# Query weights ahead of the gate weights in the ring, and the last turned rows of each head behind the next piece of work

## The chip, the core and the metric

The kernel runs on one core of a Trainium2 chip. The core has five engines that run on their own instruction lists and meet at semaphores: TensorE (PE, matrix products, PEld for its weight loads), VectorE (DVE), ScalarE (ACT), GpSimd (POOL) and SyncE (SP, which here only issues DMAs). Each engine takes its list strictly in order, so an instruction that waits holds up everything behind it. The metric is the time of one execution in microseconds on the device; the kernel before takes 2796.95 us (median of three runs, 2794.47 to 2798.68).

## The reference

The program computes two blocks in a row on 512 tokens of width 1024. The change touches only the start and the end of the heads of the first mixer of the second block, an mLSTM with 4 heads, on 512 latent and 256 context tokens:

```python
q, k, v, o, z, g = jnp.split(h @ w_in, ML_SPLITS, axis=-1)        # for latent and context rows
...                                                               # g: 16 gate columns, q and k: 256 per head
hc, st = mlstm_scan(qc, kc, vc, li_c, lf_c, zero)                 # both directions; the state goes on
hl, _ = mlstm_scan(ql, kl, vl, li_l, lf_l, st)
...
hn = _merge_heads(_head_rms(h_sum, head_g)).astype(o.dtype)       # norm over the 512 columns of a head
return (jax.nn.sigmoid(o) * hn * jax.nn.silu(z)) @ w_out
```

The input `h` is the first block's output after its final RMS norm, and after the second block's own norm and modulation.

## The kernel before, in words

**Split products.** Every large weight matrix is cut into units of at most 128 x 1024 numbers, each loaded by SP into a ring of five raw slots (`wring`). ACT rounds a unit to its high part (`wh`, L1086), POOL subtracts to get the low part (`wl`, L2234), and TensorE makes three products of high and low parts (L515 in `project`, L535 in `product`). `wh` and `wl` have only **three slots**. The function `split` on ACT waits, before it writes unit number n of the ring, until TensorE has reported the unit n - 3 as used. The order of the units is that of `weight_jobs()`, and it decides which unit waits for which. The order in which ACT and POOL work on them is written out by hand in their own programs and has to follow it.

**The start of the mixer.** After the last down projection of the first block (`dn`, to about 1410 us) TensorE makes the context half of the gate columns, takes the sum of squares of the latent rows (`norm(("mL", 0))`, a product with ones), makes the context half of the queries of head 0, takes the same for the final norm (`norm(("fin", 0))`), and then, k-tile by k-tile as the normed rows arrive, the latent halves of gates and queries (L535). Behind it stands `project_qk(0)`, the keys of head 0 (weights `("mqk", 0, 1)`, L515). Its claims wait until ACT has copied the two query tiles out of PSUM (`mqk`, L1429), since they use the same banks.

ACT at this place: squares, `root(("mL", 0))` (L1128, L1132), the high parts of the normed rows (L1114), `root(("fin", 0))` (L1128, L1132 again), then the softplus of the forget gates (L1383 to L1388), which waits for DVE's `glf` (L1918), then `split(("mqk", 0, 1))`, then the copies of the queries (L1429). DVE: the normed rows (L1679, L1687), the final norm of the first block, which needs ACT's root (L1702, 8 tiles), four memsets, the gates out of PSUM (L1916, L1918), and after the softplus the running sums and maxima of the gates (L1922 to L1945, `gfm`), for which TensorE waits after `project_qk(0)`.

**A head.** For each head: queries and keys, the row maxima of the decay matrix spread over the partitions (L876 and L565, two pairs, one for each direction, banks 4, 5 and 6, 7), the values, the scores, and in `head_pv` the product with the values, six row tiles for two directions (L855). Each row tile is normed by DVE, ACT and POOL (L1959 to L1968, L1402 to L1417, L2337) and then turned by four transposes of TensorE (L862); ACT copies the result out (L1420). The turned rows of tile t - 1 stand behind the products of tile t; those of the last tile stand at the end, with nothing ahead of them. `head_pv(h - 1)` for odd h stands behind `project_qk(h)`, and is followed by the two pairs of L876 and L565; `head_pv(h)` for odd h is followed by the first output gate unit, `("oz", 8 * f)`. An `("oz", j)` is two units of weights and four outputs: o for context and latent rows, z for both; each output runs through both units.

## Time and profile before

| what | value |
|---|---|
| median of three runs | 2796.95 us |
| the profiled execution | 2804.22 us |
| its span, first to last instruction | 2802.2 us |
| mean granted clock of TensorE | 0.967 of full speed |
| TensorE busy | 2602.1 us (93%) |
| chain that ended last | PE 85%, DVE 5%, POOL 4%, ACT 4% |

The busy shares are an average over the whole program; what matters for this change are the few places where TensorE stands still in the mLSTM part. A granted clock of 1.00 is 2.4 GHz, 0.50 is 1.2 GHz.

### The profile page before, as it was taken

How to read it: one execution, taken by the hardware profiler on the slowest of the kernel's cores; microseconds unless marked ns; L12 is line 12 of the kernel's file. 1: busy time of each engine (PE TensorE's matmuls, PEld its weight loads, DVE VectorE, ACT ScalarE, POOL GpSimd, SP SyncE). 2: the span in 40 equal slices, each digit the busy share in tenths (PEclk: the TensorE clock that was granted, in tenths of full speed). 3: DMA queues.
4: the chain of work that ended last, by engine and by line, in shares of the span. 5: the costliest groups of instructions: out<-in, count | busy, mean ns of one | idle time of the engine just before them, and what ended most of it. 6: DMA issues, size and time to landing. Idle time of an engine off the chain costs nothing.

```text
span 2802.2 us, 33854 instructions
## 1 busy us (share of the span) xinstructions
PE 2602.1 (93%) x13182; PEld 2113.0 (75%) x13182; DVE 1123.0 (40%) x2055; ACT 992.7 (35%) x1814; POOL 977.5 (35%) x515
## 2 busy tenths in 40 slices
PE   5999899999999989999989899989999998898888
PEld 4775678888777567888868778878877887786666
DVE  2135489520213658952161122420121242455564
ACT  3334344432334534443232222221222222344442
POOL 4321345765432225576532222222222223321121
PEclk9999899999999989999999999999999999899999
DMA  4211245222311115523221000211100111120000
GB/s 167 68 35 53 68 155 191 94 94 94 112 65 35 61 61 184 177 94 109 92 72 38 23 31 31 68 51 57 47 21 31 38 61 53 56 63 28 24 30 30
DMA packets 54013, 200.57 MB, mean 72 GB/s; under 512 B 5984, under 2 KB 5984, under 8 KB 52960
## 3 DMA queue, kind: packets, MB, share of 16 engines
q1 hardware_dynamic: 51696, 188.65, 20.0%
q10 hardware_dynamic: 2160, 9.76, 1.0%
q8 instruction: 106, 1.74, 0.3%
q14 instruction: 51, 0.42, 0.0%
HBM read 196.29 MB, written 2.10 MB: 71 GB/s over the span
## 4 chain that ended last, share of the span: by engine, by line
PE 85%; DVE 5%; POOL 4%; ACT 4%; issue 2%; DMA 0%; ACTq 0%; POOLq 0%; DVEq 0%
PE ps L515 53%; PE ps L535 12%; PE ps L565 8%; PE ps L855 5%; PE ps L713 3%; POOL wl L2234 2%; POOL norm_acc L2247 1%; PE ps L728 1%; PE ps L1049 1%; DVE norm_sq L1679 1%; ACT wh L1086 1%; PE ps L715 0%; POOL norm_sq L2337 0%; PE ps L862 0%; PE ps L1034 0%
## 5 line engine op out<-in xcount | busy, mean ns | idle before, releaser
L2234 POOL TENSOR_TENSOR wl<-wring,wh 128x1024 fp32r<-128x1024 f32 (+1 forms) x305 | 762.4, 2500 | 1395.1 <-ACT wh L1086 1383.9
L1086 ACT ACTIVATE wh<-wring 128x1024 fp32r<-128x1024 f32 (+1 forms) x305 | 316.8, 1042 | 743.9 <-PE ps L515 736.9
L515 PE MATMUL ps<-hh,wh 128*128 128x512 f32 x1200 | 471.6, 393 | 20.3 <-DVE hl L1691 16.0
L515 PE MATMUL ps<-hl,wh 128*128 128x512 f32 x1200 | 469.8, 392 | 0.0
L515 PE MATMUL ps<-hh,wl 128*128 128x512 f32 x1200 | 469.5, 391 | 0.0
L515 PEld LDWEIGHTS ps<-hh,wh 128*128 128x128 f32 x1200 | 227.2, 189 | 72.4 <-DVE hl L1691 15.0
L515 PEld LDWEIGHTS ps<-hh,wl 128*128 128x128 f32 x1200 | 227.0, 189 | 47.8
L515 PEld LDWEIGHTS ps<-hl,wh 128*128 128x128 f32 x1200 | 227.1, 189 | 46.0 <-issue 0.5
L565 PE MATMUL ps<-arena 128*128 128x64 f32 (+2 forms) x720 | 186.3, 395 | 14.1 <-ACT arena L1297 5.8
L1716 DVE CUSTOM_DVE_ANT_0 arena<-arena 128x1024 f32<-128x1024 f32 x96 | 185.8, 1935 | 9.0 <-DVE arena L1892 0.5
L535 PE MATMUL ps<-hh,wh 128*128 128x512 f32 (+1 forms) x408 | 171.1, 419 | 7.6 <-DVE hl L2215 3.4
L565 PEld LDWEIGHTS ps<-arena 128*128 128x128 f32 x720 | 108.7, 196 | 85.0 <-issue 57.3
L535 PE MATMUL ps<-hh,wl 128*128 128x512 f32 (+1 forms) x408 | 162.0, 397 | 0.0
L535 PE MATMUL ps<-hl,wh 128*128 128x512 f32 (+1 forms) x408 | 161.5, 396 | 0.0
L855 PE MATMUL ps<-arena 128*128 128x258 f32 (+1 forms) x672 | 150.0, 380 | 2.4 <-DVE arena L1992 2.4
L1829 DVE CUSTOM_DVE_ANT_0 arena<-ps,arena 128x128 f32<-128x128 f32 (+3 forms) x128 | 62.7, 490 | 207.1 <-PE ps L715 111.9
L855 PEld LDWEIGHTS ps<-arena 128*128 128x128 f32 x672 | 125.0, 189 | 23.0 <-issue 4.0
L1288 ACT ACTIVATE arena<-arena,st 128x128 f32<-128x128 f32 (+3 forms) x128 | 71.8, 561 | 192.3 <-DVE st L1829 192.2
L515 PE MATMUL ps<-gu_h,wh 128*128 128x512 f32 x352 | 139.7, 397 | 0.0
L515 PE MATMUL ps<-gu_l,wh 128*128 128x512 f32 x352 | 139.5, 396 | 0.0
L515 PE MATMUL ps<-gu_h,wl 128*128 128x512 f32 x352 | 139.5, 396 | 0.0
L515 PE MATMUL ps<-wh,hh 128*128 128x256 f32 x416 | 121.2, 291 | 6.1 <-POOL wl L2234 4.3
(279 smaller groups left out, 4956.0 us busy)
## 6 DMA issues: line engine op xcount, KB each, us to landing
wring<-wts SPq DMA_DIRECT2D x290, 512.0 KB, 3.5
arena<-wts SPq DMA_DIRECT2D x48, 512.0 KB, 4.3
wring<-wts SPq DMA_DIRECT2D x16, 384.0 KB, 2.9
xL<-xt SPq DMA_DIRECT2D x1, 2048.0 KB, 9.7
arena<-tab SPq DMA_DIRECT2D x1, 2048.0 KB, 16.9
arena<-cv ACTq DMA_DIRECT2D x2, 1024.0 KB, 5.6
arena<-tab ACTq DMA_DIRECT2D x1, 2048.0 KB, 9.0
out_t<-xL ACTq DMA_DIRECT2D x8, 256.0 KB, 2.0
```

The costliest lines, as they stand in the source:

```text
L515: mm = nc.tensor.matmul(o[0], a, b, start=start and k == first and j == 0, stop=stop and k == last and j == 2)
L535: mm = nc.tensor.matmul(dst, a, b, start=start and x == 0 and i == 0 and j == 0, stop=stop and x == len(us) - 1 and i == kn - 1 and j == 2)
L565: last = nc.tensor.matmul(dst, a, b, start=start and i == 0, stop=stop and i == len(pairs) - 1)
L713: last = nc.tensor.matmul(ps[:, s % 3, 0:ke], a, b, start=True, stop=kind != "fox")
L728: last = nc.tensor.transpose(ps[:, 3 + tb, 128 * j:128 * j + 128], sbuf[:, u % 4, 128 * j:128 * j + 128], idn)
L855: last = nc.tensor.matmul(ps[:, b + half, 0:c1 - c0], arena[:, eo:eo + 128], mvt[:, s, c0:c1], start=i == 0, stop=i == len(src) - 1)
L1049: last = nc.tensor.transpose(ps[:, 4 + j // 4, 128 * (j % 4):128 * (j % 4) + 128], asb[:, u % 4, 128 * j:128 * j + 128], idn)
L1086: nc.scalar.activation(wh[:, sn % SPLIT_SLOTS, :kn * w], raw(u)[:, :kn * w], ACT.Copy).then_inc(act_done, tick("act", ("hi", u)))
L1288: nc.scalar.activation(sbuf[:, s % 4, 0:ke], sbuf[:, s % 4, 0:ke], ACT.Exp, scale=-1.0, bias=mx1[:, s % 16:s % 16 + 1], accum_out=rs1[:, s ...
L1716: V.tensor_tensor_reduce(out=ada_dump, in0=raw(u), in1=crow[:, j, :], scale=1.0, scalar=0.0, op0=ALU.mult, op1=ALU.add, accum_out=modv[:, ...
L1829: V.tensor_tensor_reduce(out=sbuf[:, s % 4, 0:ke], in0=ps[:, s % 3, 0:ke], in1=bias, scale=-scale, scalar=3e38, op0=ALU.add, op1=ALU.min, ...
L2234: G.tensor_tensor(wl[:, sn % SPLIT_SLOTS, :kn * w], raw(u)[:, :kn * w], wh[:, sn % SPLIT_SLOTS, :kn * w].bitcast(F32), ALU.subtract).then_inc(
```

## The change

Three things are moved, nothing is computed otherwise.

1. In the order of the ring the gate unit goes behind the two query units of head 0. TensorE makes the first unit's half of the context queries, the sum of squares, the second half, and then the context gates. ACT splits `("mqk", 0, 0)` at the end of the down projection and the gate unit between the last squares, and `("mqk", 0, 1)` ahead of `root(("fin", 0))` instead of behind the softplus. POOL follows.
2. For even heads the transposes of the last row tile move from the end of `head_pv` to between the two pairs of L876 and L565 (`last_rows(h - 1, 0)`).
3. For odd heads they move into the middle of the first `("oz", j)`, between o and z, and to bank 4 (`last_rows(h, 4)`). That first `("oz", j)` is written out by `product` instead of `project`; both its units are reported as used by its last matmul.

```diff
@@ weight_jobs
-    add(("gate",), "ml_w_in_2", 0, 0, KT,
-        [(ML_G, 4), (None, 28), (ML_G + 8, 4), (None, 28), (ML_G + 4, 4), (None, 28), (ML_G + 12, 4)])
     for f in range(2):
         for h in (2 * f, 2 * f + 1):
             add(("mqk", h, 0), "ml_w_in_2", 0, 0, KT, [(256 * h, 256)])
+            if h == 0:
+                add(("gate",), "ml_w_in_2", 0, 0, KT, [(ML_G, 4), (None, 28), (ML_G + 8, 4), (None, 28),
+                                                       (ML_G + 4, 4), (None, 28), (ML_G + 12, 4)])
             add(("mqk", h, 1), "ml_w_in_2", 0, 0, KT, [(1024 + 256 * h, 256)])
@@ TensorE, start of the mixer
-            claim([4, 5], "dve", "glf")
-            product(ps[0:100, 4, 256:512], rows(gate_all, *hc), [gate_unit])
-            norm(("mL", 0))
             for i in range(2):
                 claim([2 * i, 2 * i + 1], "act", "mqk", 0, i)
             for u in query_units:
                 for i in range(2):
                     product(ps[:, 2 * i, 256:512], rows(side(i), *hc), [u], start=u is query_units[0],
                             stop=u is query_units[1])
+                if u is query_units[0]:
+                    norm(("mL", 0))
+            claim([4, 5], "dve", "glf")
+            product(ps[0:100, 4, 256:512], rows(gate_all, *hc), [gate_unit])
             norm(("fin", 0))
@@ TensorE, head_pv and what follows
+            def last_rows(h, b):
+
+                pe.wait_ge(pool_done, at("pool", "hn", h, NA - 1))
+                claim([b], "act", "ht", h, NA - 1)
+                for j in range(4):
+                    last = nc.tensor.transpose(ps[:, b, 128 * j:128 * j + 128],
+                                               hb[:, (NA - 1) % 2, 128 * j:128 * j + 128], idn)
+                last.then_inc(pe_done, tick("pe", ("ht", h, NA - 1)))
+
             def head_pv(h):
 
-                for t in range(NA + 1):
+                for t in range(NA):
...
                 for d in range(2):
+                    if d and h % 2:
+                        last_rows(h - 1, 0)
                     b, r = 4 + 2 * d, ROW0[d] + h
...
                     claim([b + 2, b + 3], "dve", "zz", j)
+                    if j == 8 * f:
+                        for i, key in enumerate((("o", j), ("z", j))):
+                            us = views(("oz", j))
+                            product(ps[:, 2 * i, 256:512], rows(side(i), *hc), us)
+                            product(ps[:, 2 * i + 1, :], lat(side(i)), us, key,
+                                    *([("used", x[0]) for x in us] if i else []))
+                            if i == 0:
+                                last_rows(h, 4)
+                        continue
                     project(("oz", j), both(b // 2, P, side(0), ("o", j)) + both(b // 2 + 1, P, side(1), ("z", j)))
@@ ACT
-                            split(("gate",) if last else ("cq", l + 1))
+                            split(("mqk", 0, 0) if last else ("cq", l + 1))
...
-            split(("mqk", 0, 0), first)
             square_both(6)
             square(("mL", 0), 7, ("xd", DEPTH - 1), fgn[:, 7:8])
-            split(("mqk", 0, 0), second)
+            split(("gate",))
             square(("fin", 0), 7, ("xd", DEPTH - 1))
             root(("mL", 0))
             high(("mL", 0), hH, 0)
+            split(("mqk", 0, 1))
             root(("fin", 0))
...
+                        b = t % 2 if t < NA else 4 * (h % 2)
                         nc.scalar.activation(hn[:, 4 * (h % 2):4 * (h % 2) + 4, 128 * (t - 1):128 * t],
-                                             ps[:, t % 2, :].rearrange("p (a b) -> p a b", a=4), ACT.Copy).then_inc(
+                                             ps[:, b, :].rearrange("p (a b) -> p a b", a=4), ACT.Copy).then_inc(
...
-                    if m % 2 == 0:
+                    if m % 2 == 0 and h + m:
                         split(("mqk", h, 1) if m == 0 else ("mv", h, 0))
@@ POOL
-                            split(("gate",) if last else ("cq", l + 1))
+                            split(("mqk", 0, 0) if last else ("cq", l + 1))
...
-            split(("mqk", 0, 0), slice(0, 1))
             accumulate(("mL", 0), 6)
             accumulate(("fin", 0), 6)
             accumulate(("mL", 0), 7)
-            split(("mqk", 0, 0), slice(1, 2))
+            split(("gate",))
             accumulate(("fin", 0), 7)
```

The first place is ACT at the start of the mixer. 128x800 is the gate unit, `hh` the normed rows, 128x512 from `ps` the root of the final norm, 36x768 the softplus, 128x768 the copies of queries and keys. Before:

```order
L1114 ACTIVATE hh<-norm_sq,mod 128x512 x8
L1128 ACTIVATE arena<-ps,prmt 128x512
L1132 ACTIVATE arena<-arena 128x512
L1383 ACTIVATE arena<-arena 36x768
L1385 ACTIVATE arena<-arena 36x768
L1388 ACTIVATE arena<-arena 36x768
L1086 ACTIVATE wh<-wring 128x1024 x2
L1429 ACTIVATE arena<-ps 128x768 x2
```

And now, in the same stretch (line numbers are those of the changed kernel, about 20 higher):

```order
L1134 ACTIVATE hh<-norm_sq,mod 128x512 x8
L1106 ACTIVATE wh<-wring 128x1024 x2
L1148 ACTIVATE arena<-ps,prmt 128x512
L1152 ACTIVATE arena<-arena 128x512
L1403 ACTIVATE arena<-arena 36x768
L1405 ACTIVATE arena<-arena 36x768
L1408 ACTIVATE arena<-arena 36x768
L1450 ACTIVATE arena<-ps 128x768 x2
```

The two splits of the key weights moved ahead of the root of the final norm; the copies of the queries stay behind the softplus.

The second place is TensorE at the end of head 0 (products of the last row tile, L855 before and L864 now; transposes from `norm_sq`; the two pairs from `arena` and `prmt`; then the values of head 1). Before:

```order
L855 MATMUL ps<-arena 128x256 x3
L855 MATMUL ps<-arena 128x258 x3
L862 MATMUL ps<-prmt,norm_sq 128x128 x8
L876 MATMUL ps<-arena,prmt 128x256
L565 MATMUL ps<-arena,prmt 128x512
L876 MATMUL ps<-arena,prmt 128x256
L565 MATMUL ps<-arena,prmt 128x512
L515 MATMUL ps<-wh,hc_h 128x256
```

Now:

```order
L864 MATMUL ps<-arena 128x256 x3
L864 MATMUL ps<-arena 128x258 x3
L871 MATMUL ps<-prmt,norm_sq 128x128 x4
L887 MATMUL ps<-arena,prmt 128x256
L566 MATMUL ps<-arena,prmt 128x512
L847 MATMUL ps<-prmt,norm_sq 128x128 x4
L887 MATMUL ps<-arena,prmt 128x256
L566 MATMUL ps<-arena,prmt 128x512
L516 MATMUL ps<-wh,hc_h 128x256
```

Of the eight transposes the last four went behind the first pair.

The third place is TensorE at the end of head 1, where `("oz", 0)` follows (L515 before; L536 now, since it is written out by `product`). Before:

```order
L855 MATMUL ps<-arena 128x256 x3
L855 MATMUL ps<-arena 128x258 x3
L862 MATMUL ps<-prmt,norm_sq 128x128 x8
L515 MATMUL ps<-hc_h,wh 128x256
L515 MATMUL ps<-hc_l,wh 128x256
L515 MATMUL ps<-hc_h,wl 128x256
```

Now:

```order
L864 MATMUL ps<-arena 128x256 x3
L864 MATMUL ps<-arena 128x258 x3
L871 MATMUL ps<-prmt,norm_sq 128x128 x4
L536 MATMUL ps<-hc_h,wh 128x256
...
L536 MATMUL ps<-hh,wl 128x512
L847 MATMUL ps<-prmt,norm_sq 128x128 x4
L536 MATMUL ps<-hc_h,wh 128x256
```

In the rows left out stand the rest of the 48 matmuls of o; the last four transposes now follow them, ahead of z.

## Rows read from the trace of the kernel before

**Rows 1.** The page: the chain that ended last, share of the span by engine.

```profile
PE 85%; DVE 5%; POOL 4%; ACT 4%; issue 2%; DMA 0%; ACTq 0%; POOLq 0%; DVEq 0%
```

**Rows 2.** TensorE's waits: line, who waited for, us in total, times, longest us.

```profile
PE ps L862 <- POOL norm_sq L2337: 23.7, 8, 4.2
```

**Rows 3.** Timeline of TensorE, 1410 to 1449 us: start, duration, instruction, idle time before.

```profile
1414.67 0.70 PE L565 MATMUL ps<-norm_acc,ones 128*128 128x512 f32 x1 [1.59 <-POOL norm_acc L2247]
...
1438.37 0.39 PE L535 MATMUL ps<-hh,wl 128*128 128x512 f32 x1
...
1448.82 0.55 PE L515 MATMUL ps<-hc_h,wh 128*128 128x256 f32 x1 [10.06 <-POOL wl L2234]
```

**Rows 4.** Timeline of ScalarE, 1406 to 1447 us.

```profile
1429.04 0.67 ACT L1128 ACTIVATE arena<-ps,prmt 128x512 f32<-128x512 f32 x1
...
1441.17 0.84 ACT L1383 ACTIVATE arena<-arena 36x768 f32<-36x768 f32 x1 [10.79 <-DVE arena L1918]
...
1443.67 1.99 ACT L1086 ACTIVATE wh<-wring 128x1024 fp32r<-128x1024 f32 x2
...
1445.56 1.48 ACT L1429 ACTIVATE arena<-ps 128x768 f32<-128x768 f32 x2
```

**Rows 5.** Timeline of VectorE and GpSimd, same stretch and what follows.

```profile
1430.41 5.39 DVE L1702 SCALAR_TENSOR_TENSOR xL<-xL,prmt,arena 128x512 f32<-128x512 f32 x8 [0.49 <-ACT arena L1132]
...
1460.30 0.55 DVE L1945 TENSOR_SCALAR arena<-arena 36x768 f32<-36x768 f32 x1
...
1444.79 6.60 POOL L2234 TENSOR_TENSOR wl<-wring,wh 128x1024 fp32r<-128x1024 f32 x2 [25.66 <-ACT wh L1086]
```

**Rows 6.** Timeline of ScalarE and TensorE, end of head 0.

```profile
1599.75 0.69 ACT L1402 ACTIVATE norm_sq<-ps,st 128x512 f32<-128x512 f32 x1 [3.06 <-DVE st L1963]
...
1601.40 0.60 PE L862 MATMUL ps<-prmt,norm_sq 128*128 128x128 f32 x4
...
1606.15 1.11 PE L862 MATMUL ps<-prmt,norm_sq 128*128 128x128 f32 x4 [4.16 <-POOL norm_sq L2337]
...
1607.20 1.22 PE L876 MATMUL ps<-arena,prmt 36*128 36x256 f32 x2
...
1609.92 1.06 PE L876 MATMUL ps<-arena,prmt 36*128 36x256 f32 x2
...
1612.61 0.58 PE L515 MATMUL ps<-wh,hc_h 128*128 128x256 f32 x1
```

**Rows 7.** Timeline of TensorE and ScalarE, end of head 1.

```profile
1704.78 0.60 PE L862 MATMUL ps<-prmt,norm_sq 128*128 128x128 f32 x4
...
1707.73 0.58 ACT L1420 ACTIVATE arena<-ps 128x512 f32<-128x512 f32 x1
...
1711.33 0.58 PE L515 MATMUL ps<-hc_h,wh 128*128 128x256 f32 x1 [0.69 <-ACT arena L1420]
```

**Rows 8.** The first output gates: TensorE, ScalarE, GpSimd.

```profile
1727.17 1.06 ACT L1086 ACTIVATE wh<-wring 128x1024 fp32r<-128x1024 f32 x1 [14.94 <-PE ps L515]
...
1728.31 2.40 POOL L2234 TENSOR_TENSOR wl<-wring,wh 128x1024 fp32r<-128x1024 f32 x1 [13.63 <-ACT wh L1086]
...
1729.40 0.39 PE L515 MATMUL ps<-hh,wl 128*128 128x512 f32 x1
```

**Rows 9.** Stretches: length, busy time of each engine, granted clock (PEclk), DMA.

```profile
1472.00:1473.00 1.00, 1.00 (x4) 0.26 (x2) 1.00 (x4) 0.00 (x0) 0.00 (x0) 0.79 0.00 0
1562.00:1569.00 7.00, 5.22 (x26) 3.93 (x25) 3.90 (x14) 3.33 (x9) 1.63 (x2) 1.00 0.24 76
1708.00:1709.00 1.00, 0.00 (x0) 0.00 (x0) 0.00 (x0) 0.31 (x1) 1.00 (x1) 0.55 0.00 0
1714.00:1715.00 1.00, 1.00 (x7) 1.00 (x6) 0.00 (x0) 0.00 (x0) 0.67 (x1) 0.54 0.00 0
1846.00:1848.00 2.00, 0.00 (x0) 0.00 (x0) 2.00 (x2) 1.54 (x2) 0.89 (x1) 1.00 0.14 20
1848.00:1849.00 1.00, 0.00 (x0) 0.00 (x0) 0.97 (x2) 0.00 (x0) 0.00 (x0) 0.52 0.74 229
```

More of the change, by code:

```diff
@@ L838, in project_v @@
                 project(key, outs, claims=lambda t: claim([t % 4], "act", "mv2", h, j, t) if t >= 4 else None)
+            def last_rows(h, b):
[5 more added lines that the diff above has]
+                last.then_inc(pe_done, tick("pe", ("ht", h, NA - 1)))
             def head_pv(h):
-                for t in range(NA + 1):
+                for t in range(NA):
                     for d in range(2):
-                        if t == NA:
-                            break
                         b = 4 + 2 * d
```

## The prediction, made before the changed kernel ran

> **What bounds the kernel now.** I read the chain of waits first: TensorE holds 85% of it [rows 1], so only what makes TensorE stop or slow down counts. Then its waits, summed: 23.7 us in eight waits for normed rows [rows 2]; the longest single one outside the norms is 10.06 us for the low part of a weight unit [rows 3]. Then the timeline at these places. The 10.06 us stand at the start of the mixer: the last matmul of the latent queries ends at 1438.76, the first of head 0's keys starts at 1448.82 [rows 3]. The row blames GpSimd, but that engine only starts at 1444.79 [rows 5], after ScalarE's split at 1443.67 [rows 4]; and the split stood behind the softplus, which had itself waited 10.79 us for VectorE [rows 4]. The reader should see one more thing: the copies of the queries, 1445.56 to 1447.04 [rows 4], are behind the softplus too, and the keys' banks wait for them. So two things release the keys, the weights at about 1448.7 and the banks at 1447.1. Of the eight waits for normed rows four, at the last tile of each head, are 4.16 us long [rows 6]; the other four, at the first tile, share what is left of the 23.7, 1.8 each.
>
> **Start of the mixer, up to the queries.** The gate unit's low part gives way to a second full one ahead of the sum of squares. A full unit costs GpSimd 2.40 us [rows 8], one of 800 of 1024 columns about 1.9, so the sum of squares comes some 0.6 us later (0.5, and ScalarE's high part is longer too). TensorE already waits for it there, 1.59 us [rows 3]. The same matmuls follow on both sides of it. Their end, which I call E, moves from 1438.76 to 1439.4: **+0.6 us**.
>
> **From the queries to the keys.** The split of the keys' weights now stands ahead of the final norm's root. By the three slots, its first unit waits for the first query unit, its second for the second query unit, and that is used up only by the last matmul of the stretch, at E. ScalarE therefore stands at this split until E, and the root, which ran at 1429.04 [rows 4] well ahead of E, stands behind it. From there the chain is serial, with all lengths from rows: split to root 0.95 (two splits lie between 1443.67 and 1445.56) [rows 4]; root to VectorE's first tile 1.37 (1429.04 to 1430.41) [rows 4, 5]; that to the softplus 10.76 (1430.41 to 1441.17: eight tiles of the final norm, four memsets, the gates) [rows 4, 5]; softplus 2.50 (to 1443.67) [rows 4]; the two copies 1.48 [rows 4]; 0.05 to TensorE. The sum is 17.1 us, so the keys start at 1456.5 instead of 1448.82: **+7.7 us** with the 0.6 in it. What goes is the wait for the weights (ready at about 1442.7 now); what is late next is the banks. Below these terms the chain has no slack, since each link has nothing else to wait for. The gates' running maxima end 11 us later, at about 1472.2 (1460.85 before [rows 5]); TensorE asks for them after 18.4 us of keys at 1474.9, so they add nothing, with 3 us to spare. Price if that cover went: 1 or 2 us.
>
> **Even heads, twice.** TensorE stops at 1602.0 and waits until 1606.15 [rows 6]. The first pair needs only banks 4 and 5, which ScalarE had read by 1600.44 (1599.75 + 0.69) [rows 6], so it runs inside the wait. It took 2.72 us behind the transposes (1607.20 to 1609.92) [rows 6], and the second pair as much. GpSimd's norm sets 1606.15 as before. So the values start 2.72 us earlier: **-5.4 us** for both. The nearest bounds: 1.3 us each if the pair would cost on the path only what it costs at full clock (half of 2.72), 4.9 each if the clock would also stay up over the transposes and the second pair.
>
> **Odd heads, twice.** TensorE stops at 1705.38, and the output gates start at 1711.33 [rows 7]. Now they wait for the copy that empties bank 1, tile 4 of the turned rows, which ends at 1708.31 (1707.73 + 0.58) [rows 7]: 2.97 us earlier, not 5.9. The transposes cost 0.5 us later, in the middle of dense work (four took 0.60 at full clock [rows 7]). And there is a price in the slots. The second unit of the next output gates needs the slot of this one's first unit. Before, `project` reported it used 12 matmuls before the end: ScalarE split at 1727.17, GpSimd finished at 1730.71 [rows 8], and TensorE, whose last matmul of this piece started at 1729.40 [rows 8], wanted it 12 short matmuls on (0.12 each), at 1731.05. Now both are reported at the end, 2.72 us later (12 matmuls of 0.227): ready 1733.45, wanted at 1731.05, a **new wait** of 2.4 us. Nothing hides it; behind it stand all output gates. Sum: -2.97 + 0.45 + 2.4 = -0.1, for both heads **-0.2 us**. Bounds: -2.5 each if the slot is there in time after all, +1.5 each if the banks are not free earlier and only half of the wait is recovered.
>
> **The clock.** TensorE's granted clock stayed at 1.00 (2.4 GHz) over the 1.8 us waits (1562 to 1569) and fell to 0.50 (1.2 GHz) 2.7 us after the stop at 1705.38 and 2.0 us after one at 1846.0 (idle and at 1.00 until 1848, then 0.52) [rows 9]; it also fell at 1472.8, while TensorE was busy with transposes and pairs [rows 9]. It came back at 1714.9, after 3.6 us of dense work at half speed [rows 7, 9], so a fall costs about 1.7 us. The new slot wait of 2.4 us lies between the waits that keep the clock and those that lose it; I charge half a fall for each: **+1.6 us** (0 to +3.4). The wait ahead of the output gates shrinks from 5.9 to 2.97 us, which is still longer than both falls took; I give nothing for it. The Trainium skill (TensorE: Matmul & The Clock Gate, section "HAM oscillation — how this bites in real kernels") speaks of idle gaps of a few microseconds that should be avoided, and by it both new gaps, 2.9 and 2.4 us, would be short enough to keep the clock: the sum would be that of the second rival. This trace disagrees: one fall came 2.0 us after the stop. The page's section on PE-mode transposes has them not counted as work by the clock; the fall at 1472.8 agrees.
>
> **Sum.** +7.7 - 5.4 - 0.2 + 1.6 = +3.7 us. The profiled execution took 2804.22 us, so it would take 2807.9; the median is 7.3 us below the profiled one, so I forecast 2796.95 + 3.7 = **2800.6 us**. That is 0.13% more, and a measurement of this kernel can tell about 0.2%, 5.6 us, from no change.
>
> **Rivals.** *The keys start at once* (5%): the 10.06 us are a wait for weights, as its row says, and go with them. Then -10.06 + 0.6, and 1.6 for the low clock behind them, together -11; with the other terms -15: 2782. For it speaks only the row's releaser; against it the order of ScalarE and the shared banks. It is the only case in which the moved split empties the gap. *The clock stays up* (8%): over the gaps of 2.85 and 2.97 us and the slot waits TensorE stays at 2.4 GHz. Then the even heads give 4.9 and 1.7 us of dense work at full clock, -13.2; the odd ones -0.1 - 1.7 each, -3.6; no falls at the slots. With +7.7 that is -9: 2788. For it the 1.8 us waits, against it the fall at 1472.8 and those after 2.0 and 2.7 us. The page named above would give this. *The clock gives the deferrals back* (slower, 17%): it comes back at the moment at which it would have come back anyway, however much earlier the dense work starts. Then half of each advance is lost, 1.36 at the even heads and 1.5 at the odd ones: +7.7 - 2.7 + 2.8 (2.97 / 2 against 0.45 + 2.4), and both slot waits with a full fall, +3.4, is +11: 2808. Slower by over 0.2% from +5.6 us, which needs two of these three. Half of it is what the trace cannot exclude, since it shows dense work behind each fall at one distance only.
>
> **Numbers.** Forecast 70%: between -2 and +5.5, 2795 to 2802.5, with the slot wait missing (-6.4 of the sum, 2794) among it. Faster in two rivals, 12% with a small part of the forecast's lower edge. Slower: 17% and the upper edge, together 19%. That leaves 69% within 0.2%. The range of 8 in 10 goes from 2789, the clock's rival, to 2807, most of the slower one.
>
> **What would show it.** Right: the gap ahead of the keys is about 17 us and ends with ScalarE's copy (L1450), not GpSimd; ScalarE's split of the second key unit starts with the last query matmul, and the root behind it; the pair runs within 1.4 us of the stop at the even heads and the values start 2.7 us sooner; the output gates start about 3 us after the stop; and a wait of 2.4 us for the low part stands 1.4 us into the second output gate, in heads 1 and 3. Wrong: a gap ahead of the keys below 10 us, or no new wait in the output gates. If the sum is off with all these gaps in place, the clock is the term.

## The result, and the profile after

Nineteen executions of each kernel, taken side by side: the changed kernel 2802.25 us (2799.09 to 2807.50), the kernel before 2795.82 us (2792.75 to 2804.12). The ratio is 1.0024, with a 95% interval from 1.0016 to 1.0031: 6.4 us slower, between 4.5 and 8.7. The forecast was +3.7 us (2800.6). The measured difference lies beyond the band that the forecast gave itself (-2 to +5.5) and just beyond +5.6, which the prediction named as the least that could be told from no change; it is inside the range of 8 in 10. The absolute 2802.25 us falls into the band up to 2802.5 only because the kernel before now took 2795.82 us instead of 2796.95.

The profiled execution of the changed kernel took 2800.15 us, its span is 2798.2 us, and its mean granted clock 0.970. That is shorter than the profiled execution of before (2804.22 us), though the kernel is slower. So the two traces must not be compared by their totals; the section on the repetitions explains the difference.

I read the views in the same order as for the kernel before. The chain of waits first, by engine [rows 1]: TensorE has one point more, GpSimd one less. On the page of the changed kernel:

```profile
PE 86%; DVE 5%; ACT 4%; POOL 3%; issue 2%; DMA 0%; ACTq 0%; DVEq 0%; POOLq 0%
```

The waits of TensorE (line, who is waited for, us in total, times, longest us). The long one for a weight unit [rows 3] is replaced by one for ScalarE's copy:

```profile
PE ps L516 <- POOL wl L2255: 23.0, 15, 3.3
...
PE ps L516 <- ACT arena L1450: 18.4, 1, 18.4
```

The timeline of TensorE shows where each one stands (start, duration, instruction, idle time before it in brackets):

```profile
1402.91 0.39 PE L516 MATMUL ps<-gu_h,wl 128*128 128x512 f32 x1
...
1408.39 1.13 PE L566 MATMUL ps<-norm_acc,ones 128*128 128x512 f32 x2 [1.02 <-POOL norm_acc L2268]
...
1432.16 0.39 PE L536 MATMUL ps<-hh,wl 128*128 128x512 f32 x1
1450.92 0.55 PE L516 MATMUL ps<-hc_h,wh 128*128 128x256 f32 x1 [18.37 <-ACT arena L1450]
...
1569.15 0.66 PE L871 MATMUL ps<-prmt,norm_sq 128*128 128x128 f32 x4 [1.78 <-POOL norm_sq L2357]
...
1602.69 0.69 PE L887 MATMUL ps<-arena,prmt 36*128 36x256 f32 x2
...
1606.92 0.66 PE L847 MATMUL ps<-prmt,norm_sq 128*128 128x128 f32 x4 [2.67 <-POOL norm_sq L2357]
1607.51 0.69 PE L887 MATMUL ps<-arena,prmt 36*128 36x256 f32 x2
...
1609.42 0.58 PE L516 MATMUL ps<-wh,hc_h 128*128 128x256 f32 x1
...
1706.34 0.35 PE L536 MATMUL ps<-hc_h,wh 128*128 128x256 f32 x1 [3.03 <-ACT arena L1441]
...
1728.81 0.39 PE L516 MATMUL ps<-hc_h,wh 128*128 128x256 f32 x1 [2.20 <-POOL wl L2255]
```

Four of the forecast's marks can be seen. The keys wait 18.37 us and are released by ScalarE's copy. The first pair of L887 and L566 for head 1 (L887 at 1602.69) runs ahead of the wait at the end of head 0, which shrinks from 4.16 [rows 6] to 2.67 us. The output gates start after 3.03 us instead of after 5.9. And there is a new wait of 2.20 us for a low part in the second output gate; it recurs at 2213.61 with 2.21 us.

### The profile page after: what moved, and what is told of

The parts are those of the page before. It is cut to its first block, busy times and chain, and to the rows that moved or that the text cites. A ratio compares the mean times of both kernels' runs of the same rounds, so it can differ in the third digit from the quotient of the medians.

```text
span 2798.2 us, 33854 instructions
## 1 busy us (share of the span) xinstructions
PE 2591.7 (93%) x13182; PEld 2109.3 (75%) x13182; DVE 1119.3 (40%) x2055; ACT 992.1 (35%) x1814; POOL 973.8 (35%) x515
## 4 chain that ended last, share of the span: by engine, by line
PE 86%; DVE 5%; ACT 4%; POOL 3%; issue 2%; DMA 0%; ACTq 0%; DVEq 0%; POOLq 0%
PE ps L516 52%; PE ps L536 14%; PE ps L566 8%; PE ps L864 5%; PE ps L714 3%; POOL wl L2255 2%; POOL norm_acc L2268 1%; PE ps L729 1%; PE ps L1069 1%; ACT wh L1106 1%; DVE norm_sq L1700 1%; PE ps L716 0%; PE ps L1054 0%; PE ps L1053 0%; DMA prmt<-prm 0%
## 5 line engine op out<-in xcount | busy, mean ns | idle before, releaser
L516 PE MATMUL ps<-hh,wh 128*128 128x512 f32 x1168 | 458.9, 393 | 20.8 <-DVE hl L1712 16.0
L516 PE MATMUL ps<-hl,wh 128*128 128x512 f32 x1168 | 456.8, 391 | 0.0
L516 PE MATMUL ps<-hh,wl 128*128 128x512 f32 x1168 | 456.5, 391 | 0.0
L516 PEld LDWEIGHTS ps<-hh,wh 128*128 128x128 f32 x1168 | 220.8, 189 | 71.7 <-DVE hl L1712 15.0
L516 PEld LDWEIGHTS ps<-hh,wl 128*128 128x128 f32 x1168 | 220.6, 189 | 46.3
L516 PEld LDWEIGHTS ps<-hl,wh 128*128 128x128 f32 x1168 | 221.0, 189 | 44.9 <-issue 0.5
L566 PE MATMUL ps<-arena 128*128 128x64 f32 (+2 forms) x720 | 187.1, 397 | 13.9 <-ACT arena L1317 5.8
L536 PE MATMUL ps<-hh,wh 128*128 128x512 f32 (+1 forms) x440 | 183.4, 417 | 8.1 <-DVE hl L2236 3.4
L536 PE MATMUL ps<-hh,wl 128*128 128x512 f32 (+1 forms) x440 | 174.0, 395 | 0.0
L536 PE MATMUL ps<-hl,wh 128*128 128x512 f32 (+1 forms) x440 | 173.5, 394 | 0.0
L566 PEld LDWEIGHTS ps<-arena 128*128 128x128 f32 x720 | 109.6, 198 | 84.3 <-issue 57.9
L864 PE MATMUL ps<-arena 128*128 128x258 f32 (+1 forms) x672 | 149.9, 380 | 2.4 <-DVE arena L2013 2.4
L864 PEld LDWEIGHTS ps<-arena 128*128 128x128 f32 x672 | 125.0, 189 | 23.0 <-issue 4.0
```

The costliest lines, as they stand in the source:

```text
L516: mm = nc.tensor.matmul(o[0], a, b, start=start and k == first and j == 0, stop=stop and k == last and j == 2)
L536: mm = nc.tensor.matmul(dst, a, b, start=start and x == 0 and i == 0 and j == 0, stop=stop and x == len(us) - 1 and i == kn - 1 and j == 2)
L566: last = nc.tensor.matmul(dst, a, b, start=start and i == 0, stop=stop and i == len(pairs) - 1)
L864: last = nc.tensor.matmul(ps[:, b + half, 0:c1 - c0], arena[:, eo:eo + 128], mvt[:, s, c0:c1], start=i == 0, stop=i == len(src) - 1)
```

## From the queries to the keys: which link was longer

ScalarE and VectorE after the change, to be laid beside [rows 4, 5]. First ScalarE:

```profile
1432.65 1.06 ACT L1106 ACTIVATE wh<-wring 128x1024 fp32r<-128x1024 f32 x1 [7.14 <-PE ps L536]
1433.61 0.67 ACT L1148 ACTIVATE arena<-ps,prmt 128x512 f32<-128x512 f32 x1
...
1446.68 0.84 ACT L1403 ACTIVATE arena<-arena 36x768 f32<-36x768 f32 x1 [11.74 <-DVE arena L1939]
...
1449.18 1.48 ACT L1450 ACTIVATE arena<-ps 128x768 f32<-128x768 f32 x2
```

Then VectorE and GpSimd in the same stretch:

```profile
1434.97 6.34 DVE L1723 SCALAR_TENSOR_TENSOR xL<-xL,prmt,arena 128x512 f32<-128x512 f32 x8 [11.49 <-ACT arena L1152]
```

```profile
1433.78 2.34 POOL L2255 TENSOR_TENSOR wl<-wring,wh 128x1024 fp32r<-128x1024 f32 x1 [5.81 <-ACT wh L1106]
```

ScalarE stands 7.14 us at the split of the second key unit, until the last query matmul (1432.16 + 0.39 = 1432.55), and the root is behind it. From there each link can be set against the forecast: stop to split 0.10 (forecast 0), split to root 0.96 (0.95), root to VectorE 1.36 (1.37), VectorE to softplus 11.71 (10.76), softplus 2.50 (2.50), copies 1.48 (1.48), copies to TensorE 0.26 (0.05). The sum is 18.37 against 17.1. Of the 1.26 us that were missed, 0.95 are the eight tiles of the final norm: 6.34 us instead of 5.39 [rows 5]; 0.21 more stand between the last copy and TensorE. GpSimd's low part of the very unit that ScalarE has just split runs from 1433.78 to 1436.12, beside the first of these tiles; before, GpSimd was idle there. The Trainium skill (SBUF — State Buffer, section "Who interferes with whom") states that a VectorE instruction with two inputs in SBUF and a GpSimd instruction that reads SBUF exclude each other. The trace agrees: in the 1.15 us in which both ran (1434.97 to 1436.12), VectorE lost 0.95. The last kernel of experiment 4 tests it.

## Experiment 1: each part alone

The ring order alone, with the last rows of each head where they were (the edit against the changed kernel, shortened; `last_rows` goes too):

```diff
-                for t in range(NA):
+                for t in range(NA + 1):
...
-                    if d and h % 2:
-                        last_rows(h - 1, 0)
...
-                    if j == 8 * f:
-                        for i, key in enumerate((("o", j), ("z", j))):
...
-                        b = t % 2 if t < NA else 4 * (h % 2)
+                        b = t % 2
```

> The kernel before with the first part of the change alone: gate unit behind the query units in the ring, ScalarE's split of the keys' weights ahead of the final norm's root; the turned rows stay where they were. Theory (ScalarE stands at the split until the last query matmul, and root, gates, softplus and the copies that free the banks stand behind it): TensorE's gap ahead of head 0's keys is 18.4 us as in the changed kernel, ends with ScalarE's copy, and the program takes 7.5 to 8 us more than before, about 2803.5; slower than the changed kernel by 2 to 6 us. Rival (the deferred rows are the loss, the ring is neutral): within 2 us of before.

Measured: 2811.6 us, ratio 1.0036 (1.0022 to 1.0050), about 10 us more than before, where 7.5 to 8 were expected. The gap is as expected:

```profile
1457.85 0.55 PE L516 MATMUL ps<-hc_h,wh 128*128 128x256 f32 x1 [18.37 <-ACT arena L1432]
```

The last rows alone, parts two and three together, with the ring as before (again against the changed kernel, shortened):

```diff
+    add(("gate",), "ml_w_in_2", 0, 0, KT,
+        [(ML_G, 4), (None, 28), (ML_G + 8, 4), (None, 28), (ML_G + 4, 4), (None, 28), (ML_G + 12, 4)])
...
-            if h == 0:
-                add(("gate",), "ml_w_in_2", 0, 0, KT, [(ML_G, 4), (None, 28), (ML_G + 8, 4), (None, 28),
-                                                       (ML_G + 4, 4), (None, 28), (ML_G + 12, 4)])
...
-            split(("mqk", 0, 1))
```

> The kernel before with the deferred rows alone; ring, splits and queries as before. Theory: the gap ahead of the keys stays at 10.06 us, the waits at the heads' ends shrink as in the changed kernel (4.16 to 2.67 at the even heads, with the first pair inside; 5.9 to 3.0 at the odd ones, with a new wait of 2.2 for a slot), which from the two traces is -2.8, -0.1, -2.5 and -0.7 us: 4 to 7 us less than before, about 2790. Rival (the clock gives the deferrals back): within 2 us of before or slower.

Measured: 2794.37 us, ratio 0.9980 (0.9969 to 0.9991), about 5.6 us less, as expected. The 10.06 us ahead of the keys are back, and the waits of 2.68, 3.03 and 2.20 us in the heads are all there.

```profile
1443.22 0.55 PE L515 MATMUL ps<-hc_h,wh 128*128 128x256 f32 x1 [10.06 <-POOL wl L2253]
```

So the change is a loss and a gain put together: the first part costs about 0.36%, parts two and three give 0.20%. From the last matmul of the down projection to the end of the span, the stretch that holds the whole change, it is 1402.57 us for the ring alone and 1385.55 for the rows alone; three profiles of the kernel before have 1391.28 in the mean. Of the 11.3 us of the ring alone, 9.1 stand at the start of the mixer; the rest is spread over stretches behind it in which nothing was moved. Parts two and three were not run apart from each other.

## Experiment 2: is the gap the order of ScalarE?

If so, the gap must fall when the root goes ahead of the split, with the ring order kept:

```diff
+            root(("fin", 0))
             split(("mqk", 0, 1))
-            root(("fin", 0))
```

> The changed kernel with one swap on ScalarE: the root of the final norm again ahead of the split of the keys' weights. Theory (the root behind the split is the loss): the root runs at about E - 9 us as before, VectorE's gates are there 2.4 us after E (E is the end of the last query matmul), then softplus 2.5 and copies 1.5: the gap is 6.4 us instead of 18.4, and the program takes 10 to 13 us less than the changed kernel, about 2791. Rival (the ring's order itself is the loss, since the keys' second unit can only be split at E): the gap stays above 10 us and the time within 3 us of the changed kernel.

Measured: 2790.57 us, ratio 0.9962 (0.9949 to 0.9975). The three rows that follow are TensorE, VectorE and GpSimd of this kernel:

```profile
1442.92 0.55 PE L516 MATMUL ps<-hc_h,wh 128*128 128x256 f32 x1 [8.56 <-ACT arena L1450]
...
1425.78 7.53 DVE L1723 SCALAR_TENSOR_TENSOR xL<-xL,prmt,arena 128x512 f32<-128x512 f32 x8 [0.49 <-ACT arena L1152]
...
1427.39 2.72 POOL L2255 TENSOR_TENSOR wl<-wring,wh 128x1024 fp32r<-128x1024 f32 x1 [13.77 <-ACT wh L1106]
```

The gap loses 9.81 us by one swapped line: the root behind the split is what lengthened it. It ends 2.2 us later than I expected since the eight tiles now take 7.53 us: here the whole subtraction of GpSimd lies beside them, and it takes 2.72 us itself instead of 2.34.

The other half of the reading was that the copies of the queries stand behind the softplus for no reason of their own. In the kernel with the root first, both are now copied ahead of it (shortened):

```diff
+            def take_mqk(h, m):
+                act.wait_ge(pe_done, at("pe", "mqk", h, m))
+                nc.scalar.activation(mqk[:, m, :], psf[:, 1024 * (m % 2) + 256:1024 * (m % 2) + 1024],
+                                     ACT.Copy).then_inc(act_done, tick("act", ("mqk", h, m)))
+            take_mqk(0, 0)
+            take_mqk(0, 1)
...
-                    act.wait_ge(pe_done, at("pe", "mqk", h, m))
...
+                    if h or m > 1:
+                        take_mqk(h, m)
```

> As the one with the root first, and the two copies of the queries ahead of the softplus on ScalarE. Theory (the banks are what the keys wait for): the copies end 2.5 us after E, the gap is 2.6 us and ends with a copy; TensorE reaches the gate columns 4 us sooner, where it may now wait up to 3 us for the running maxima; 2 to 5 us less than with the root first, about 2787. Rival (weights, not banks): the gap stays at 4 us or more and ends with GpSimd's low part.

Measured: 2787.85 us, ratio 0.9951 (0.9938 to 0.9965). The timeline of TensorE:

```profile
1435.77 0.36 PE L516 MATMUL ps<-hc_h,wh 128*128 128x256 f32 x1 [2.81 <-ACT arena L1404]
1455.11 1.53 PE L828 MATMUL ps<-prmt,arena 128*128 128x128 f32 x6 [2.50 <-DVE arena L1972]
```

What is late next shows itself. The keys start 5.75 us sooner than in the kernel with the root first, and the first transposes of the gate columns (L828) then wait 2.50 us for the running maxima, as expected. But not all of that is new: with the root first, TensorE waits at the same place for ScalarE's copy of the keys, and so it does in both kernels of the comparison (1.06 us at 1468.26 before, at 1470.58 after).

```profile
1462.67 0.85 PE L828 MATMUL ps<-prmt,arena 128*128 128x128 f32 x6 [1.06 <-ACT arena L1450]
```

So 1.44 of the 5.75 us come back. And the maxima are late here for a reason that can be read on VectorE and GpSimd:

```profile
1451.51 2.95 DVE L1970 TENSOR_TENSOR arena<-arena 36x768 f32<-36x768 f32 x1
...
1451.13 2.53 POOL L2261 TENSOR_TENSOR wl<-wring,wh 128x1024 fp32r<-128x1024 f32 x1 [6.29 <-ACT wh L1106]
```

The addition that takes 2.95 us beside GpSimd's next subtraction takes 0.95 us in the kernel with the root first (L1964 at 1452.88), where GpSimd is idle. No run held that subtraction back. The prediction had 3 us to spare for the maxima in the changed kernel; there were 7.1 (they end at 1462.42, the keys' matmuls at 1469.53).

## Experiment 3: what do the two slot waits cost?

The first output gate reports each of its two units as used when that unit's own last matmul is done, not both at the end:

```diff
-                            product(ps[:, 2 * i + 1, :], lat(side(i)), us, key,
-                                    *([("used", x[0]) for x in us] if i else []))
+                            product(ps[:, 2 * i + 1, :], lat(side(i)), us[:1], *([("used", us[0][0])] if i else []),
+                                    stop=False)
+                            product(ps[:, 2 * i + 1, :], lat(side(i)), us[1:], key,
+                                    *([("used", us[1][0])] if i else []), start=False)
```

> The changed kernel, with the first unit of the first output gates reported as used after its own last matmul (12 matmuls before the end, as project does) instead of with the second. Theory (the new 2.2 us waits in the second output gates are for this slot): both waits go, GpSimd's low part is again there in time, and the program takes 4 us less than the changed kernel, about 2798. Rival (the wait comes from GpSimd or ScalarE being late for another reason, such as the table load or the moved copy of the turned rows): the waits stay at 2 us.

Measured: 2796.03 us, ratio 0.9993 (0.9983 to 1.0002). Both waits are gone. From the wait of 1.78 us in head 1 to the wait for `g_l` the changed kernel needs 179.6 us in each of three profiles, this one 177.13; for head 3 it is 179.6 to 179.7 against 177.15. So a slot wait costs 2.5 us in its own stretch, near its own length. Behind the down projection the whole is 1389.05 us against 1395.7 in the mean for the changed kernel: 6.7 us less, of which 5.0 stand in these two stretches; the rest is taken up below, under the clock. The clock did not fall at the slot wait in the changed kernel (windows: length, busy PE, PEld, DVE, ACT, POOL, granted clock, DMA share, GB/s):

```profile
1708.00:1711.00 3.00, 3.00 (x15) 2.98 (x15) 0.00 (x0) 0.00 (x0) 0.00 (x0) 0.52 0.00 0
...
1726.00:1729.00 3.00, 0.80 (x7) 0.59 (x6) 0.50 (x1) 2.97 (x4) 2.34 (x1) 1.00 0.00 0
1729.00:1731.00 2.00, 2.00 (x15) 1.89 (x15) 1.97 (x3) 1.11 (x2) 0.81 (x1) 1.00 0.55 164
```

Compare the first row with the other two: behind the 3.03 us wait that ended at 1706.34 the clock is at 1.2 GHz, behind the 2.20 us wait it stays at 2.4. The Trainium skill (TensorE: Matmul & The Clock Gate, section "HAM oscillation — how this bites in real kernels") has idle gaps beyond a few microseconds as the ones to avoid; both gaps here are shorter than the length that it gives, so by it both would keep the clock. The trace agrees for 2.20 us and not for 3.03.

## Experiment 4: all of it together, and two that did not pay

The kernel with the root first, the copies ahead of the softplus and the units reported early:

> The kernel with root first and copies first, and the early report of the slot as well. Theory: the gains add up, since they lie at different places of TensorE's chain: 4 us less than the one with the copies first, about 2784, 14 to 17 us less than before. Rival (a wait removed in one place comes back at the next one): within 2 us of the one with the copies first.

Measured: 2778.30 us, ratio 0.9921 (0.9907 to 0.9936). It beats both kernels, by 0.8% the one before (22 us by the ratio; 19.4 by the stretch behind the down projection, 1371.88 us against a mean of 1391.28). That is more than the 14 to 17 us expected: against the kernel with the copies first it gains 9.6 us behind the down projection, not 4. Of these, 5.0 stand in the two stretches with the slots, and 2.6 between the keys and head 0's first wait, where both kernels have the same code and TensorE's busy time at half clock is 3.0 us here against 6.3. So part of the 19.4 us is where the clock happened to fall in this profile. What still waits at the start of the mixer:

```profile
1442.28 0.55 PE L516 MATMUL ps<-hc_h,wh 128*128 128x256 f32 x1 [2.81 <-ACT arena L1406]
...
1461.77 0.88 PE L828 MATMUL ps<-prmt,arena 128*128 128x128 f32 x6 [1.36 <-DVE arena L1974]
```

That last wait, 1.36 us where 1.06 stand in any case, was to shrink by putting four of the eight final-norm tiles behind the gates on VectorE:

```diff
-            scaled(("fin", 0), lambda m: col("fin", m), xL)
+            scaled(("fin", 0), lambda m: col("fin", m), xL, range(0, 4))
...
+            scaled(("fin", 0), lambda m: col("fin", m), xL, range(4, KT))
```

> As the one with all three, and on VectorE four of the eight tiles of the first block's final norm behind the gates instead of ahead of them. Theory: the 2.5 us for which TensorE then waits for the running maxima shrink to about 0.7, since the softplus can start as soon as the copies are done; 1 to 2 us less than with all three. Rival (the running maxima are late for GpSimd's sake, whose low parts hold VectorE's scans up): the wait stays above 2 us.

Measured: 2783.17 us, ratio 0.9929 (0.9915 to 0.9944): the same as the kernel above it within the intervals. Behind the down projection it takes 1372.02 us against 1371.88. VectorE and GpSimd show why:

```profile
1441.11 3.83 DVE L1958 TENSOR_TENSOR_SCAN arena<-arena 4x768 f32<-4x768 f32 x1
...
1447.98 1.75 DVE L1958 TENSOR_TENSOR_SCAN arena<-arena 4x768 f32<-4x768 f32 x1
```

```profile
1434.96 8.36 POOL L2264 TENSOR_TENSOR wl<-wring,wh 128x1024 fp32r<-128x1024 f32 x2 [5.47 <-ACT wh L1108]
```

The gates' first scan now runs beside GpSimd's second subtraction, and takes 3.83 us there against 1.75 for the same form 7 us later; the two subtractions take 5.30 and 2.92 us instead of 2.34 each. The running maxima are in time all the same, and the wait ahead of the gate columns falls from 1.36 to 1.06 us and ends with ScalarE's copy, as in the kernels without a wait for the maxima. But the lengthened low part of a key unit is late now: a wait of 0.88 us that the kernel above did not have costs more than the 0.30 removed.

```profile
1440.32 0.39 PE L516 MATMUL ps<-hc_h,wh 128*128 128x256 f32 x1 [0.88 <-POOL wl L2264]
...
1456.79 0.85 PE L828 MATMUL ps<-prmt,arena 128*128 128x128 f32 x6 [1.06 <-ACT arena L1406]
```

Last, the changed kernel with GpSimd's low part held back until the eight tiles are done, to test what lengthened them:

```diff
-                split(("mqk", h, 1))
+                if h:
+                    split(("mqk", h, 1))
+                else:
+                    split(("mqk", 0, 1), slice(0, 1))
+                    pool.wait_ge(dve_done, at("dve", "h", ("fin", 0), KT - 1))
+                    split(("mqk", 0, 1), slice(1, 2))
```

> The changed kernel, where GpSimd makes the low part of the keys' second unit only when VectorE has finished the eight tiles of the final norm. The low part is then ready about 10 us after E, the end of the last query matmul, still well ahead of the banks. Theory (the 6.34 us of these tiles in the changed kernel instead of 5.39 are GpSimd's work beside the first of them, and this is what my sum for the gap lacked): the tiles take 5.4 us, the gap 17.4 instead of 18.4 us; in time 1 us less than the changed kernel, which the runs can hardly tell. Rival (the tiles are slower because ScalarE and TensorE stopped, or by chance): 6.3 us and 18.4 us again.

Measured: 2801.67 us, ratio 1.0007 (0.9998 to 1.0016). TensorE and VectorE:

```profile
1450.24 0.55 PE L516 MATMUL ps<-hc_h,wh 128*128 128x256 f32 x1 [17.42 <-ACT arena L1450]
...
1435.24 5.39 DVE L1723 SCALAR_TENSOR_TENSOR xL<-xL,prmt,arena 128x512 f32<-128x512 f32 x8 [11.49 <-ACT arena L1152]
```

The tiles take 5.39 us again, exactly as in [rows 5], and the gap is 0.95 us shorter. That GpSimd lengthened them is shown. The whole gains 0.1 to 0.8 us behind the down projection (1395.22 against 1395.29 to 1395.99), too little for the timed runs. Yet its ratio to before is lower than the changed kernel's (1.0007 against 1.0024), and it comes from another round with other runs of before. So between rounds the ratio of two nearly equal kernels moved by more than either interval shows, and the 6.4 us of the result are known less well than their interval says.

## Experiment 5: how much of this is the execution, not the kernel?

The two traces at hand contradicted the timed runs: behind the last matmul of the down projection the changed kernel took only 2.9 us more, while its median was 6.4 us higher; and ahead of that point, where TensorE's work is the same in both kernels, it was 6.9 us ahead (1402.91 against 1409.84). Both kernels were therefore profiled twice more, unchanged.

> The kernel before, unchanged, profiled once more. Theory (one clock fall in layer 0's attention, between 230 and 243 us, comes or does not by chance): this profile either repeats 2804.2 us with 0.50 over that stretch and the last matmul of the down projection at about 1409.8 us, or is some 6 us shorter (about 2797 to 2798) with 1.00 there and that matmul at 1403 to 1404. Rival (the fall belongs to the kernel's own code): before always has 0.50 there.

> As the first repetition of the kernel before: whichever group of times it falls in, the stretch behind the down projection is to be 1392.4 us long within 1 us, if the change's cost read from two single profiles (+2.9 us) is to stand. If it varies by 3 us or more, that cost is not known to better than that.

> The changed kernel, unchanged, profiled once more. Theory: either 2800 us with the clock at 1.00 between 230 and 243 us, or about 2806.5 to 2807.5 with 0.50 there, and behind the down projection the same 1395.3 us in both. Rival: the 6 us between its two groups of times lie somewhere behind the down projection.

> As the first repetition of the changed kernel: the stretch behind the down projection 1395.3 us within 1 us. If the longer cost of the timed runs (+6.4 us) is right and the profiles' +2.9 us is chance, repetitions of before are to show 1389 us or those of after 1399 us.

They took 2797.89 and 2795.46 us (before), 2801.89 and 2806.24 us (after). The granted clock in two stretches of about 13 us of the first block's attention, one in each of its two layers: first the kernel before, first profile and first repetition, then the second repetition of the changed kernel.

```profile
230.00:243.00 13.00, 13.00 (x23) 4.86 (x24) 4.26 (x18) 5.76 (x19) 0.61 (x1) 0.50 0.00 0
918.00:932.00 14.00, 11.90 (x39) 4.97 (x38) 9.97 (x35) 8.52 (x26) 0.61 (x1) 1.00 0.12 39
```

```profile
230.00:243.00 13.00, 12.91 (x53) 6.78 (x53) 7.30 (x28) 8.50 (x26) 0.61 (x1) 1.00 0.26 93
```

```profile
230.00:243.00 13.00, 13.00 (x53) 6.58 (x51) 7.54 (x28) 8.74 (x28) 0.61 (x1) 1.00 0.32 114
918.00:932.00 14.00, 13.72 (x24) 5.49 (x25) 5.06 (x21) 6.11 (x19) 0.61 (x1) 0.52 0.01 2
```

The same code runs at half clock in some executions and at full clock in others, of the same kernel. Where the clock falls, all that follows is 4.4 to 6.2 us later (1409.84 against 1403.62 and 1404.51 before, 1408.41 against 1402.91 and 1404.04 after, at the last matmul of the down projection). My expectation was right about the kind of event and wrong about its place: the slower repetition of the changed kernel had it in the second layer, not in the first. It fits the two groups into which the times of one kernel fall: 12 of the changed kernel's 19 lie between 2799.1 and 2802.6 us, 7 between 2806.0 and 2807.5. The timed runs have no trace, only a mean granted clock, and it agrees: 0.967 or 0.968 in the 7, 0.969 to 0.971 in the 12. Of before's 19, 15 lie below 2798.7 and 4 above 2800.2; the profile on which the forecast rests was of the upper group. Within the lower groups the medians differ by 5.8 us (2801.47 and 2795.63).

With three profiles of each, the stretch that holds the change can be divided at TensorE's rows. Each number is the start of one row less the start of the one before it; the borders are the last matmul of the down projection, the first of the keys, the waits of 1.78 us in the four heads, and the two waits for `g_l` ahead of the output products.

| stretch | before, us | after, us | means | forecast |
|---|---|---|---|---|
| down projection to keys | 38.98, 38.97, 38.97 | 48.01, 48.02, 48.06 | +9.1 | +7.7 |
| keys to head 0's wait | 119.56, 118.05, 118.08 | 118.23, 118.61, 118.66 | -0.1 | 0 |
| to head 1's wait (even end) | 103.38, 103.55, 102.05 | 100.55, 101.43, 101.50 | -1.8 | -2.7 |
| to `g_l` (odd end, gates) | 179.72, 180.33, 179.56 | 179.61, 179.63, 179.62 | -0.2 | -0.1 + 0.8 |
| to head 2's wait | 202.81, 203.08, 202.82 | 203.36, 203.17, 203.27 | +0.4 | 0 |
| to head 3's wait (even end) | 104.35, 104.55, 104.25 | 101.85, 101.62, 101.64 | -2.7 | -2.7 |
| to `g_l` (odd end, gates) | 180.29, 180.41, 180.24 | 179.63, 179.65, 179.62 | -0.7 | -0.1 + 0.8 |
| to the end of the span | 463.27, 463.34, 463.22 | 464.05, 463.73, 463.62 | +0.5 | 0 |
| sum | 1392.36, 1392.28, 1389.19 | 1395.29, 1395.86, 1395.99 | +4.4 | +3.7 |

The waits themselves are the same in every profile of the changed kernel (18.37, 2.67, 3.03 and 2.20 us, within 0.01). What varies is the clock behind them, and with it 3.2 us of the sum: my condition, 1 us, was not met by the kernel before, whose second repetition has 1389.19, the value that I had named as the sign that the cost of +2.9 us is chance. At the end of head 0 this can be seen directly. In the first profile of before the values started 6.46 us after the wait's end (1606.15 to 1612.61 [rows 6]); in its first repetition 5.60:

```profile
1598.41 0.66 PE L862 MATMUL ps<-prmt,norm_sq 128*128 128x128 f32 x4 [4.16 <-POOL norm_sq L2337]
...
1604.01 0.58 PE L515 MATMUL ps<-wh,hc_h 128*128 128x256 f32 x1
```

After the change it was 2.50 us in the first profile (above, 1606.92 to 1609.42) and 3.90 in its first repetition:

```profile
1608.44 1.11 PE L847 MATMUL ps<-prmt,norm_sq 128*128 128x128 f32 x4 [2.67 <-POOL norm_sq L2357]
...
1612.34 0.58 PE L516 MATMUL ps<-wh,hc_h 128*128 128x256 f32 x1
```

Four transposes take 0.66 us where the fall comes after them, and 1.11 where it came before. At the end of head 2 it is 6.46, 6.45 and 6.46 us before, and 3.90 three times after: 2.56 us saved, where the forecast had 2.72.

What stays open: the repeated profiles give +4.4 us, the timed runs +6.4 with 4.5 as the lower end of the interval, and another round put a nearly equal kernel at +0.07% (-0.02 to +0.16), about 2 us. The pair of profiles with the largest difference gives 6.8 (1395.99 less 1389.19), so differences in where the clock falls are able to make up the rest, and the larger share of the upper group in the changed kernel's runs (7 against 4) adds to a median; which of the two it is was not separated, nor whether the change has any part in how often the clock falls in the first block, where the code is the same.

## Why the prediction held, step by step

**Start of the mixer, up to the queries.** The sum of squares waits less (1.02 us instead of 1.59 [rows 3]), but a new wait of 0.98 us stands right behind the down projection (it ends at 1404.29; by its row it is for GpSimd's low parts of the query units, which are both done at 1404.06). The prediction did not have it. The last query matmul starts 29.25 us after the down projection instead of 28.53. That is +0.7, forecast +0.6.

**From the queries to the keys.** The mechanism is right in every link: the split starts with the last query matmul, the root behind it, the keys with the copy. Swapping the two lines (gap of 8.56 us) and moving the copies (2.81 us) each took its link out of the gap. The term of the sum that was mis-sized is this one: +9.1 against +7.7. I had taken VectorE's eight tiles from a row in which GpSimd stood idle, and did not ask what the split that I had just moved ahead of them would start on GpSimd. Holding GpSimd back gave the 5.39 us back. The cover of the running maxima held, with 7.1 us to spare instead of 3: their scans had lain beside GpSimd's subtractions before (3.21 us for the scan of 4x512) and no longer do (1.27).

**Even heads.** The pair runs in the wait, the wait's end is set by GpSimd as before, and the values start 2.56 us sooner at head 2. At head 0 the saving is 0.6 to 3.0 us by the pair of profiles, -1.8 in the mean. Together -4.5 against -5.4; the part at head 0 is where the clock falls.

**Odd heads.** Output gates 2.9 us sooner (wait 3.03 instead of 5.95), slot wait 2.20 (forecast 2.4) at a cost of 2.5. Together -0.9 against -0.2. TensorE is busy at half clock for 3.4 us in each of these stretches, before for 4.3 to 6.1, which is of the size of the difference. Without the slot waits 2.5 us more would have been saved for each, which experiment 3 shows; that this price came with the way the units are reported was read rightly from the order of the ring.

**The clock.** The term of +1.6 did not occur: the clock stood at 1.00 through both slot waits in the trace. In its place +0.9 appeared in two stretches in which nothing was moved. The kernel with the rows alone has them too (203.40 and 463.66 us), the ring alone does not (203.12 and 463.36), and without the slot waits they are gone (202.74 and 462.59). What differs in them is TensorE's busy time at half clock: 3.2 to 4.1 us before, 4.2 to 4.9 after and 3.4 without the slot waits in the first of them; 38.5 to 39.9, 41.2 to 42.1 and 36.8 us in the second. The second stretch takes 463.6 to 464.1 us in all seven profiles with slot waits, and 462.5 to 462.7 in the three where they were taken away. So the slot waits did have a price in clock, but far behind them. Why the falls lie differently there was not found. For both slot waits and their clock the prediction had 6.4 us; without them the changed kernel needs 6.7 us less, so the total was about right and its parts were not.

**The rivals.** The keys did not start at once: the gap grew. The clock did not stay up over 2.67 and 3.03 us. The third rival, the deferrals given back, can be seen at head 0 alone: by the two repetitions the values start 1.7 and 1.5 us sooner there, against 2.72 forecast and 1.36 by the rival, and by the first pair of profiles 3.96 us sooner, 2.8 of them left at head 1's wait. At head 2 it is 2.56 each time. Its price of two full falls at the slot waits did not come.

So +3.7 is the sum of terms that missed by +1.4, +0.9, +0.8, -0.7 and -1.6 (start, even heads, the unmoved stretches, odd heads, clock), measured by the profiles, which give +4.4. That they nearly cancel was luck, and each one alone is better evidence than the total.

## What to carry to other kernels

In a ring with few slots, an order of loads is also an order of waits on every engine that fills the slots: before a unit is moved forward, look at whose "used" it must wait for, and keep everything that other engines need ahead of that wait in the list. Here one line below such a wait was worth 10 us, and copies that stood behind an unrelated wait another 6, of which 1.4 came back at the next wait. When a step is moved beside a VectorE chain on the path, read that chain's price from a row in which GpSimd is as busy as it will be; and compare kernels by the stretch that holds the change, over several profiles, when total times differ by less than what one chance clock fall costs. A small difference of medians is worth a second round.

## What the runs showed that I had not expected

One clock fall, in code that no kernel here touches, made all that followed 4.4 to 6.2 us later and came in 4 of 14 profiles (three times at 230 us, once at 918 us). Eight VectorE tiles of 128x512 took 5.39, 6.34 or 7.53 us with none, 1.15 us or all of one GpSimd subtraction of 128x1024 beside them, and a scan of 4x768 took 3.83 instead of 1.75 us. The 2.20 us waits left the clock alone in all three traces of the changed kernel. At the 2.67 us waits it fell every time, five times of six within the wait and once 1.6 us after its end; at the 3.03 us waits every time 0.5 to 1.1 us after the end.
